# Layer MLP of a two-layer diffusion backbone: partial sums, squares and conditioning products placed differently

## The reference, cut to what matters

```
mods = jnp.split(jax.nn.silu(cvec) @ lp['w_ada'] + lp['b_ada'], 6, axis=-1)
sh1, sc1, g1, sh2, sc2, g2 = [m[:, None, :] for m in mods]
...
x = x + g1 * rms_norm(mix, lp['g_post1'])
h = rms_norm(x, lp['g_pre2']) * (1.0 + sc2) + sh2
f = jnp.square(jax.nn.relu(h @ lp['w_mlp1'])) @ lp['w_mlp2']
x = x + g2 * rms_norm(f, lp['g_post2'])
```

## Time and profile before

| | us |
|---|---|
| median of three runs | 3509.28 |
| lowest, highest | 3502.06, 3510.10 |
| the profiled execution | 3516.75 |
| its span | 3514.9 |
| layer 0's MLP, first Relu to the end of its down projection, about | 765 to 1910 |
| layer 1's MLP, about | 2435 to 3507 |

### The profile page before, as it was taken

One profiled execution on the slowest core, in us unless ns is written; L12 is line 12 of the kernel. 1 busy time (PEld: TensorE's weight loads), 2 busy tenths in 40 slices (PEclk: granted clock), 3 DMA queues, 4 the chain that ended last, 5 costly groups with the idle time before them and its releaser, 6 DMA issues.

```text
span 3514.9 us, 51258 instructions
## 1 busy us (share of the span) xinstructions
PE 3274.1 (93%) x17787; PEld 2856.9 (81%) x17787; DVE 2219.1 (63%) x3500; ACT 1160.6 (33%) x1671; POOL 775.1 (22%) x481
## 2 busy tenths in 40 slices
PE   5899988979999999999998898997999999999998
PEld 2588755768989889898897897676998998998997
DVE  1358654389889898998979498756334334334334
ACT  2122322243333333332333332434333333333332
POOL 0048022032121221212210285322111111111110
PEclk7799998989999999999999899998999999999999
DMA  8865567546666656666563333122444443443442
GB/s 289 285 204 170 164 204 233 167 138 192 205 201 213 200 190 208 210 210 192 186 215 120 123 108 106 61 85 67 131 127 125 130 126 126 131 126 125 131 126 96
DMA packets 479418, 566.33 MB, mean 161 GB/s; under 512 B 17688, under 2 KB 395152, under 8 KB 478896
## 3 DMA queue, kind: packets, MB, share of 16 engines
q1 hardware_dynamic: 476992, 560.02, 50.1%
q0 software_dynamic: 1344, 4.33, 0.4%
q10 hardware_dynamic: 944, 0.32, 0.0%
HBM read 560.93 MB, written 3.67 MB: 161 GB/s over the span
## 4 chain that ended last, share of the span: by engine, by line
PE 68%; DVE 13%; issue 10%; DMA 5%; ACT 3%; SPq 1%; DVEq 0%; POOL 0%; ACTq 0%; POOLq 0%
PE ps L1351 34%; PE ps L1359 26%; DVE ada_sums L1278 6%; DMA ada_raw<-in_w_ada_dram 4%; PE ps L1435 2%; DVE w_lo L842 1%; PE ps L1599 1%; ACT w_hi L563 1%; DVE conv L1053 1%; DVE h_lo L933 1%; DMA raw<-in_w_in_dram 1%; PE ps L1465 1%; PE ps L1573 1%; PE ps L1587 1%; ACT facc L604 1%
## 5 line engine op out<-in xcount | busy, mean ns | idle before, releaser
L842 DVE TENSOR_TENSOR w_lo<-raw,w_hi 128x1024 fp32r<-128x1024 f32 x660 | 919.9, 1398 | 858.5 <-ACT w_hi L563 849.6
L563 ACT ACTIVATE w_hi<-raw 128x1024 fp32r<-128x1024 f32 x672 | 710.2, 1058 | 1394.8 <-PE ps L1351 706.2
L1351 PE MATMUL ps<-h_hi,w_hi 128*128 128x384 f32 x2816 | 959.4, 341 | 27.9 <-DVE h_lo L933 24.1
L1351 PE MATMUL ps<-h_lo,w_hi 128*128 128x384 f32 x2816 | 950.7, 338 | 0.0
L1351 PE MATMUL ps<-h_hi,w_lo 128*128 128x384 f32 x2816 | 950.5, 338 | 0.0
L1278 DVE SCALAR_TENSOR_TENSOR ada_sums<-ada_raw,cond,ada_sums 128x256 f32<-128x256 f32 x1440 | 648.2, 517 | 7.3 <-issue 7.3
L1359 PE MATMUL ps<-w_hi,hid_hi 128*128 128x512 f32 x1536 | 609.0, 396 | 9.3 <-issue 7.4
L1359 PE MATMUL ps<-w_hi,hid_lo 128*128 128x512 f32 x1536 | 605.3, 394 | 0.0
L1359 PE MATMUL ps<-w_lo,hid_hi 128*128 128x512 f32 x1536 | 604.6, 394 | 0.0
L1351 PEld LDWEIGHTS ps<-h_hi,w_hi 128*128 128x128 f32 x2816 | 535.9, 190 | 46.3 <-issue 39.9
L1351 PEld LDWEIGHTS ps<-h_lo,w_hi 128*128 128x128 f32 x2816 | 535.6, 190 | 0.9
(11 more groups left out here) (193 smaller groups left out, 2391.8 us busy)
## 6 DMA issues: line engine op xcount, KB each, us to landing
raw<-in_w_mlp_dram SPq DMA_DIRECT2D x512, 512.0 KB, 3.9
ada_raw<-in_w_ada_dram SPq DMA_DIRECT2D x384, 512.0 KB, 4.9
raw<-in_w_in_dram SPq DMA_DIRECT2D x96, 512.0 KB, 4.3
raw<-in_w_out_dram SPq DMA_DIRECT2D x64, 512.0 KB, 4.3
out_dram<-x SPq DMA_DIRECT2D x6, 512.0 KB, 2.7
x<-in_x_sample_dram SPq DMA_DIRECT2D x1, 2048.0 KB, 10.1
pw_w<-in_w_conv_pw_dram POOLq DMA_DIRECT2D x2, 1024.0 KB, 5.9
x<-in_x_prompt_dram SPq DMA_DIRECT2D x1, 1024.0 KB, 5.0
```

The source lines that it names most:

```text
L563: nc.scalar.activation(w_hi[:, j % 4, :, :], raw[:, j % 4, :, :], ACT.Copy).then_inc(hi_ready, 1)
L842: nc.vector.tensor_tensor(w_lo[:, j % 4, :, :], raw[:, j % 4, :, :], w_hi[:, j % 4, :, :].bitcast(F32), ALU.subtract).then_inc(lo_ready, 1)
L1351: last = nc.tensor.matmul(ps[:, 2 * pair + t, 0:TOK], w[:, j % 4, k, P * t:P * t + P], v[:, kt + k, :], start=begin and k == 0 and i == 0, ...
```

## The change

In the MLP loop of both layers GpSimd has no work left but to clear `facc` once.

- **Partial sums.** `copy_acc`, `stage` and GpSimd's addition are gone. VectorE adds each bank to `facc` itself (`add_acc`), three instructions of 512 columns per down quad in chunks 0 to 6, placed ahead of `w_lo` of unit 3. TensorE waits for them (`acc_added`) where it waited for ScalarE's copies.
- **Squares.** ScalarE does Relu, Square into `z[18:20]`, and then a Copy into `hid_hi`; all three stand ahead of `w_hi` of unit 3.
- **Conditioning products.** A load brings 256 rows x 512 columns in place of 512 x 256. A block of 512 columns is made over two product quads (`wide` loads, b even and odd), 4 products of 512 columns per unit. There is one buffer of sums: the first product of a block waits for the turn of the block before. A turn takes 8 matmuls, after unit 1 of quads 2, 5 and 7 (`WIDE_TURN`), three per chunk in place of six. In down quads the products of unit 2 come behind the additions.
- VectorE waits for the cleared `facc` before its loop.

The core of the diff:

```
+WIDE_TURN = {2: 0, 5: 1, 7: 2}
...
-                with pool.Fori(0, CHUNKS - 1) as ch:
-                    hidden_squares(ch)
-                    for n in range(4):
-                        pool.wait_ge(acc_copied, ch * 12 + (84 * layer + 3 * n + 6))
-                        dst = facc[:, place(n), :, :]
-                        nc.gpsimd.tensor_tensor(dst, dst, stage[:, :, :], ALU.add).then_inc(added, 1)
...
-                    act.wait_ge(sqh_ready, hidden + (32 * layer + 1))
                     nc.scalar.activation(z[:, 16:18, :], ps[:, 2 * pair:2 * pair + 2, 0:TOK], ACT.Relu).then_inc(acc_free, 1)
                     act.wait_ge(acc_free, blk(layer, B_MLP + 1) + ch * B_CHUNK + b)
-                    nc.scalar.activation(hid_hi[:, bass.ds(tile, 2), :], z[:, 16:18, :], ACT.Square).then_inc(hidh_ready, 1)
+                    act.wait_ge(hid_ready, hidden + (32 * layer + 1))
+                    nc.scalar.activation(z[:, 18:20, :], z[:, 16:18, :], ACT.Square).then_inc(sqh_ready, 1)
+                    act.wait_ge(sqh_ready, hidden + (32 * layer + 1))
+                    nc.scalar.activation(hid_hi[:, bass.ds(tile, 2), :], z[:, 18:20, :], ACT.Copy).then_inc(hidh_ready, 1)
...
+                def ada_products(ch, b, j, mark0):
+                    n, k0 = ch * 6 + (ADA_BLOCKS + b), mark0 + 3 * (4 * b + j)
+                    begin = b % 2 == 0 and j == 0
                     dve.wait_ge(ada_landed[j], 16 * (n + 1))
+                    if begin:
+                        dve.wait_ge(ada_turned, ch * 3 + (ADA_BLOCKS + b // 2))
+                    for o in range(4):
                         k, g = divmod(o, 2)
+                        out, src, by = ada_sums[:, g, :], wide(ada_raw, j)[:, k, :], cond[:, 8 * (b % 2) + 2 * j + k, g:g + 1]
...
+                            op = nc.vector.scalar_tensor_tensor(out=out, in0=src, scalar=by, in1=out, op0=ALU.mult, op1=ALU.add)
+                        op.then_inc(ada_used if o == 3 else dve_chain, 1)
+
+                def add_acc(ch, n, t):
+                    i = ch * 12 + (84 * layer + 3 * n + t)
+                    if t < 2:
+                        dve.wait_ge(acc_done, ch * 8 + (56 * layer + 2 * n + t + 1))
+                    else:
+                        dve.wait_ge(unit_used, ch * (4 * Q_CHUNK) + 4 * quad(layer, Q_MLP + 4 + n) + 4)
+                    dve.wait_ge(acc_added, i + 3)
+                    dst = facc[:, place(n), t, :]
+                    nc.vector.tensor_tensor(dst, dst, ps[:, BANK_ACC + t, :], ALU.add).then_inc(acc_added, 1)
 
                 def mlp_quad(ch, k, mark0, adds=None):
+                    products = first and k + 1 in ADA_OF_QUAD
+                    late = products and k >= 4
                     for j in range(4):
                         if k == 3 and j == 3:
                             hidden_low(2 * k, ch * 4 + (k + 32 * layer))
                         if adds and j == 3:
                             adds()
+                            if late:
+                                ada_products(ch, ADA_OF_QUAD[k + 1], 2, mark0)
                         w_low(j, ch * Q_CHUNK + quad(layer, Q_MLP + k + 1))
```

## The result

The changed kernel takes 3476.78 us (median of 5 runs, 3468.92 to 3480.71) against 3509.28 before: ratio 0.9905, 95% interval 0.9889 to 0.992, a gain of 32.5 us. The forecast was 3460 in a range of 3440 to 3487, a gain of 49.6. So sign and range held, but a third of the gain is missing: the time lies just outside the band of 3450 to 3475 that had a chance of 0.60, in the one of 3475 to 3499 that had 0.15.

What follows compares the result with a forecast made beforehand. TensorE was taken as the bound, with layer 0 losing time to late products. Seven chunks at 138.4 instead of 144.98 give 46.1 us; with + 0.3 - 0.4 + 4.0 - 0.4, 49.6 off 3509.28: 3460 us, range 3440 to 3487.

Steps and rivals of the forecast that it cites:

- What bounds it: MLP loops: TensorE's own time bounds layer 1, nothing to win there; 13.1 us a chunk to be won in layer 0.
- GpSimd's hold: Layer 0's loop: GpSimd's squares and additions stretch VectorE's rows; removing them gives back 13.4 us of VectorE's time a chunk.
- the product's price: VectorE's 512-column conditioning products: 0.665 us from start to start, four per unit, 12.5 us a chunk less.
- u = 3.0: Time of a unit's four products on VectorE if each waits for an empty pipe; rejected in favour of 2.66 us.
- The additions: VectorE adding PSUM banks, three per down quad: 0.60 us apart, 7.2 us of VectorE's time a chunk.
- 131.9 + 5.1 + 0.6 + 0.25 + 0.6: Layer 0's chunk, us: TensorE's work, three turns, late bank after k = 6, late bank at k = 5, late turn at k = 2.
- the likeliest case: Whole kernel: 3460 us, within 3450 to 3475, chance 0.60; its short holds of 0.6 us bring no low clock.
- The last chunk: Layer 0's last chunk: up part gains 0.3 us, first down quad loses 0.4, three down quads gain 4.0.
- The load sum: VectorE's net load in layer 0: 13.4 + 12.5 - 7.2 = 18.7 us a chunk less.
- little is left: Rival: at u = 3.0 longer holds and one low clock make layer 0's chunk 143.8, kernel 3497 us; 3475 to 3499, chance 0.15.
- slower: Rival: accumulator hand-off becomes the bound at u = 3.18, chunk 149, kernel 3533 us; chance 0.05.
- more: Rival: turns at 0.92 us and no hold, chunk 134.7, kernel 3433 us, half-way 3447; chance 0.15.

Runs made afterwards that it cites:

- e3: The changed kernel, with GpSimd again making additions of the old sizes, in spare rows that nobody reads: 3548.67 us, ratio 1.0125.
- e4: The changed kernel with the turn of quad k = 2 one unit later, after its third unit: 3466.57 us, ratio 0.9878.
- e8: The changed kernel with every product except the two that begin a block cut to 16 of 512 columns, output not the reference's: 3450.39 us, ratio 0.9835.
- e9: The changed kernel with the turn of quad k = 2 one unit earlier, after its first unit: 3533.43 us, ratio 1.0064.
- e1: The changed kernel with the old 256-column products and six turns per chunk, GpSimd still out of the loop: 3491.84 us, ratio 0.9955.
- e7: The changed kernel with later turns (quads 2, 4, 6), products in VectorE's quads 0 to 5 and a second pair of sums: 3459.13 us, ratio 0.9849.
- e2: The kernel before with only the 512-wide products and their three turns per chunk, GpSimd's squares and additions kept: 3509.39 us, ratio 0.9997.
- e6: The kernel of e3 (GpSimd adding in spare rows) with its three turns one unit later: 3516.41 us, ratio 1.0014.

## Why the prediction was right in sign and short in size

**What bounds it, held.** Layer 1 didn't move, and the 13.1 us a chunk were layer 0's. 5.5 of them are the turns, which stayed; the others were pauses ahead of turns and the low clock behind them, and of these 7.6 the change took 5.1. GpSimd's hold (e3), the product's price (four in 2.73 at 0.744, so 0.66 apart; forecast 0.665) and with it the rejection of u = 3.0 held. The additions came at (2.12 - 0.69) / 2 = 0.72 apart and not 0.60, which costs 12 x 0.12 = 1.4 us of VectorE a chunk, most of it unseen.

**The chunk.** The forecast 131.9 + 5.1 + 0.6 + 0.25 + 0.6 = 138.4 stands against the chunks without low clock: 131.9, three turns at 18.46 - 16.64 = 1.82 (5.5, forecast 5.1), 0.61 at the turn of k = 2 (0.6), nothing at k = 5 (0.25), 0.77 at the bank after k = 6 (0.6): 138.8, measured 138.7. This is 0.3 above the forecast, 2.3 us in seven chunks. As idle time the rows show less than was forecast, 0.34 us at the turn and 0.47 at the bank; what the other 0.3 us of either are isn't shown.

**The step that failed** is in the likeliest case's assumption, "idle gaps of 2.8 us have brought it, mine are 0.6": I gave the low clock behind a short hold 15% and left it out of the sum. It came in five of seven chunks, 5 x 1.55 = 7.8 us, and e4, e8 and e9 show that the pause ahead of that turn is its cause. (Not every pause is one: those of 1.2 to 1.5 us at the banks in e1 left the clock at 1.00.) With the 2.3 it makes the loop's miss of 46.1 - 36.0 = 10.1 us.

**The last chunk.** Forecast a gain of 0.3 - 0.4 + 4.0 and a loss of 0.4 in layer 1, 3.5 in all; measured a loss of 1.75 in close 0 and 0.1 in the rest, 5.4 us off. The down quads did gain (from the last Relu to quad 6's end 64.1 became 62.0 us), and so the 4.0 was 2.1; then the turn in the close, which I had not looked at, waits 3.35 us and runs at the low clock, in 3.58 us; before, it waited 2.35 and took 1.02 at the full clock, which fell only behind it. e7 takes that away and gets 5.3 us back against e4. The up half lost 1.1 us to the low clock at k = 2, where 0.3 of gain was forecast.

10.1 and 5.4 are 15.5 of the 17.1 us between forecast and median; the rest is within the spread of the runs.

**The parts.** The load sum treated GpSimd's 13.4 us and the width's 12.5 as shares of VectorE's time, and time isn't gained in such shares: 18 us by the one alone, 0 by the other. The stretches say where. In the loop e1 gives 29.6 us, e2 2.9 and the change 36.0, so most of the loop's gain comes with GpSimd's removal, in either order (29.6 without the width, 33.1 with it). VectorE has to reach the turn of quad 7 in time; with GpSimd's hold in quad 6 it doesn't, whatever is saved in other quads (e2). Without the hold the narrow products leave 3.3 us a chunk, the two waits at the banks (e1), and the wide ones 2.5, the short holds and the low clock at k = 2. The rest of what e1 lacks is in the last chunk (5.2 us lost, 2.3 in the change) and in the spread between executions. From there on more relief gives little: e8 takes another (780.30 - 463.19) / 7 = 45 us a chunk off VectorE and gains 0.8 over e4.

The rivals: "little is left" and "slower" rested on u, and u was 0.66. The first one's other half, a hold that brings the clock down, is what happened, at 1.55 us instead of 3.0. Of "more" nothing came; turns cost their 1.82.

## What to carry to other kernels

An engine's relief is worth what it changes at the next point where someone waits for it; take the parts of a change one by one past that point before adding them up. When TensorE waits for another engine, even for a third of a microsecond as at the turn here, look at the granted clock behind the wait, and move the waiting matmuls behind work that is ready: here one line (e4) gave 10 us. And look at the last pass of a loop by itself, where an operation that is covered inside may have nothing behind it.

## What the hardware showed that I had not expected

- The low clock can follow pauses much shorter than the 2.8 us that I knew. At the turn of k = 2: none in e4, e7 and e8 without a pause (7 chunks each); behind 0.34 us in five of seven, for 1.55 us; behind 0.93 (e3) in five of seven, for 1.56; behind 4.50 in all, for 3.2 to 3.9. In e2 it came behind 0.16 us in two of seven.
- The length of the pause doesn't decide alone. Ahead of the 512-column matmuls that wait for a bank, the clock stayed at 1.00 behind 0.47 us (changed kernel, seven of seven) and behind 1.18 and 1.5 us (e1, 14 of 14); it fell behind 2.86 us in four of seven (e3) and behind 3.62 in seven of seven (e6). The turn in quad 6 of the kernel before, behind 0.27 us, left it at 1.00 in all seven. What makes the turn of k = 2 so sensitive, and what decides between chunks whose rows read alike, isn't settled. One chunk of e2 had a quad 5 of 20.03 us instead of 18.39 without an idle row ahead of its turn, so a pause isn't the only thing that can bring it.
- GpSimd slows VectorE with no data between them: 2.5 us for an addition of 3.11 in spare rows.
- TensorE's turn of a 512-wide block, eight matmuls of one column, costs 1.82 us, twice the 0.92 of four; by width alone nothing is saved there.
